# Loads, GLU tiles, sample states and chunks of a hybrid decoder step in another order, and expert rows in slots four apart

## The reference

```python
proj = xn @ w_in                               # z, xBC, dt, u
xbc, new_conv = _causal_conv(xbc, conv_prefix, conv_w, conv_b)
y, new_ssm = _ssd_chunked(xs, dt, -jnp.exp(a_log), bm, cm, d_ssd, ssm_h0, chunk)
y_ssd = _rmsnorm(y * jax.nn.silu(z), ssd_norm)
y_s5, new_re, new_im = _s5_group(u, ...)       # Re(C h) + D u, gelu, y * sigmoid(y @ w_glu), norm
x = x + jnp.concatenate([y_ssd, y_s5], axis=-1) @ w_out
x = x + _hier_moe(_rmsnorm(x, norm_ffn), ...)  # 4 groups x 8 experts, top 2 of one group
...
for e in range(MOE_EXPERTS):
    h = jax.nn.silu(t @ w_gate[e]) * (t @ w_up[e])
    out = out + gates[:, e:e + 1] * (h @ w_down[e])
```

## Time and profile before

| | us |
|---|---|
| median of 3 runs | 1102.85 |
| lowest, highest | 1101.57, 1104.02 |
| profiled execution | 1102.73 |
| its span | 1100.9 |
| TensorE busy | 992.9 (90%) |
| VectorE busy | 441.0 |
| ScalarE busy | 311.5 |
| GpSimd busy | 330.2 |
| waits of L650 for weights | 13.8 |
| L650, all wide tiles, busy | 273.1 |

### The profile page before, as it was taken

One profiled execution on the slowest core, in us unless ns is written; L12 is line 12 of the kernel. 1 busy time (PEld: TensorE's weight loads), 2 busy tenths in 40 slices (PEclk: granted clock), 3 DMA queues, 4 the chain that ended last, 5 costly groups with the idle time before them and its releaser, 6 DMA issues.

```text
span 1100.9 us, 16994 instructions
## 1 busy us (share of the span) xinstructions
PE 992.9 (90%) x6438; PEld 701.5 (64%) x6439; DVE 441.0 (40%) x674; ACT 311.5 (28%) x597; POOL 330.2 (30%) x534
## 2 busy tenths in 40 slices
PE   6999989999999999999999999999977778998881
PEld 5889768876876587999765555555544434554440
DVE  6999874353435699963151111111101011111103
ACT  3026222453202625322242222222212121221223
POOL 1000888888012994000012222222221111221210
PEclk9999999999979899999989999999989999999996
DMA  6684261110529643327299999999999999999954
GB/s 259 124 146 74 42 141 40 39 60 20 62 79 264 235 150 132 136 96 296 111 359 377 395 392 390 384 393 408 399 393 409 381 421 411 411 417 414 423 237 162
DMA packets 73564, 277.54 MB, mean 252 GB/s; under 512 B 36952, under 2 KB 38872, under 8 KB 56496
## 3 DMA queue, kind: packets, MB, share of 16 engines
q1 hardware_dynamic: 63020, 252.67, 62.6%
q0 software_dynamic: 8720, 19.86, 6.6%
q10 hardware_dynamic: 1780, 4.41, 1.1%
HBM read 260.17 MB, written 25.61 MB: 260 GB/s over the span
## 4 chain that ended last, share of the span: by engine, by line
PE 54%; DMA 22%; DVE 17%; SPq 3%; issue 2%; ACT 1%; POOLq 0%; ACTq 0%; POOL 0%; DVEq 0%
DMA sb_arena<-w_up 16%; PE ps L650 11%; PE ps L1015 8%; PE ps L1008 7%; PE ps L1029 7%; PE ps L912 7%; DVE sb_arena L1386 6%; DMA sb_arena<-w_gate 4%; SPq L407 2%; PE ps L982 2%; PE ps L769 2%; PE ps L795 1%; PE ps L820 1%; PE ps L738 1%; PE ps L816 1%
## 5 line engine op out<-in xcount | busy, mean ns | idle before, releaser
L650 PE MATMUL ps<-sb_arena 128*128 128x264 f32 (+1 forms) x1152 | 273.1, 398 | 14.7 <-DMA sb_arena<-wi 13.8
L650 PEld LDWEIGHTS ps<-sb_arena 128*128 128x128 f32 x1152 | 222.1, 194 | 65.9 <-DMA sb_arena<-wi 13.9
L1889 DVE TENSOR_TENSOR sb_s5b<-sb_s5b,ps 128x256 f32<-128x256 f32 x36 | 22.4, 623 | 414.4 <-PE ps L1015 414.4
L1015 PE MATMUL ps<-sb_arena 128*64 128x256 f32 x1152 | 134.5, 387 | 21.3 <-DMA sb_arena<-w_up 21.3
L1008 PE MATMUL ps<-sb_arena 128*64 128x256 f32 x1152 | 134.3, 387 | 19.1 <-DMA sb_arena<-w_gate 15.0
L1029 PE MATMUL ps<-sb_arena 128*64 128x512 f32 x576 | 131.5, 598 | 20.6 <-DVE sb_arena L1893 20.6
L1008 PEld LDWEIGHTS ps<-sb_arena 128*64 128x64 f32 x1152 | 84.3, 139 | 79.7 <-DMA sb_arena<-w_gate 24.4
L1015 PEld LDWEIGHTS ps<-sb_arena 128*64 128x64 f32 x1152 | 83.6, 139 | 68.3 <-DMA sb_arena<-w_up 27.4
L1359 ACT ACTIVATE sb_kxf<-ps,sb_gate_of 64x512 f32<-64x512 f32 x36 | 24.6, 682 | 304.9 <-PE ps L1029 304.9
L1029 PEld LDWEIGHTS ps<-sb_arena 128*64 128x64 f32 x576 | 39.0, 136 | 90.0 <-issue 61.0
L606 POOL COPY sb_idc<-sb_tok_of 64x1 int32 x36 | 6.4, 178 | 288.5 <-DMA sum_scr<-sb_kxf,sb_rwc 272.4
...
...
## 6 DMA issues: line engine op xcount, KB each, us to landing
...
sb_arena<-wi SPq DMA_DIRECT2D x28, 512.0 KB, 4.1
...
sb_arena<-wglu SPq DMA_DIRECT2D x8, 512.0 KB, 4.6
sb_arena<-ssm_in POOLq DMA_DIRECT2D x8, 512.0 KB, 15.3
o_ssm_s<-sb_arena POOLq DMA_DIRECT2D x8, 512.0 KB, 4.9
```

Source lines behind the costliest of these rows:

```text
L650: last = mm(ps[:, b0 + h, 0:t1 - t0], ring[w % 3][:, k, :], src[:, k, t0:t1], start=k == 0, stop=k == KD - 1)
L1015: last = mm(ps[64 * r:64 * r + 64, 1, 0:256], xt[:, k, :], Wu[s][:, k, 256 * r:256 * r + 256], start=k == 0, stop=k == KD - 1)
L1889: V.tensor_tensor(hh.rearrange("p (j c) -> p c j", j=2), sg.rearrange("p (c j) -> p c j", j=2), ps[:, 1, 0:256].rearrange("p (c j) -> p c ...
```

## The change

- The sync engine issues `ring_load(14)` after `toeplitz(0)` and 15 after `toeplitz(1)`; `y_load(0)` comes before `y_store(1)`.
- TensorE: `wide(25)` goes ahead of `state_outputs(0, 8)`, which now follows chunk 2's `ssd_y_off` and waits for `yo_ev` 4; `wide(27)` goes ahead of `ssd_c(3)`, `wide(28)` ahead of chunk 4, `wide(29)` ahead of `ssd_c(4)`. Tile 27 leaves bank 0 for the alternating pair.
- GpSimd loads samples 4 to 7 after the eighth round of state_outputs, bcf after the sixteenth, and samples 0 to 3 when all of `y_store(1)` has landed (`y5_st[1]`).
- VectorE: `off_diagonal` joins Yo and the decay of the carried state, ahead of the mask product (in chunk 4 ahead of the scaled inputs). The S5 additions 0 to 7 go into chunk 2 ahead of its y, 8 to 15 behind its states. Samples 0, 1, 2 are done in chunk 3 ahead of its y, 3, 4, 5 behind its states, 6 and 7 in chunk 4 ahead of its y. `project_out(3)` comes ahead of `root_inverse(1)`, `project_out(4)` between the two halves of `scale_s5`.
- ScalarE: the gelus come ahead of `b_tokens(4)` and `segment_exp(4)`, with a one-element Exp behind them, and read contiguous columns but write strided ones. The squares 4 to 7 move from tile 33 to 32.
- The slots: rank r = 16 e + w of a tile goes to slot 4 w + e.

```diff
         def wide_bank(w):
-            return 0 if 20 <= w < 28 else 2 * (w % 2)
+            return 0 if 20 <= w < 27 else 2 * (w % 2)
...
             toeplitz(0)
+            ring_load(14)
             toeplitz(1)
-            ring_load(14)
+            ring_load(15)
...
-            y_store(1)
             sp.wait_ge(y5_st[0], 16 * 9)
             y_load(0)
+            y_store(1)
             sp.wait_ge(y5_st[1], 16 * 9)
...
+            pl.wait_ge(y5_mm, 8)
+            for b in range(4, NS):
+                pl.dma_start(h0b[b], hin[b]).then_inc(h0s_ld[1], 16)
             pl.wait_ge(ea_out, 1)
             pl.wait_ge(y5_mm, 16)
...
-            for b in range(NS):
-                pl.dma_start(h0b[b], hin[b]).then_inc(h0s_ld[b // 4], 16)
+            pl.wait_ge(y5_st[1], 16 * 9)
+            for b in range(4):
+                pl.dma_start(h0b[b], hin[b]).then_inc(h0s_ld[0], 16)
...
             wide(24)
-            state_outputs(0, 8)
             ssd_a(2)
...
             wide(25)
+            pe.wait_ge(yo_ev, 4)
+            state_outputs(0, 8)
             ssd_c(2)
...
             wide(26)
+            pe.wait_ge(yo_ev, 6)
+            wide(27)
             ssd_c(3)
-            wide(27)
+            wide(28)
             ssd_a(4)
             ssd_b(4)
             ssd_y_off(4)
-            wide(28)
+            pe.wait_ge(yo_ev, 8)
+            wide(29)
             ssd_c(4)
-            for w in range(29, 36):
+            for w in range(30, 36):
...
+                if c == 2:
+                    s5_add(0)
+                for b in ((0, 1, 2) if c == 3 else (6, 7) if c == 4 else ()):
+                    sample_c(b)
                 dv.wait_ge(y_mm, c + 1)
...
+                if c == 2:
+                    s5_add(8)
                 if c == 3:
-                    sample_c(0)
-                    sample_c(1)
-            for b in range(4, NS):
-                sample_c(b)
+                    for b in range(3, 6):
+                        sample_c(b)
...
+            project_out(3)
             root_inverse(1)
             scale_s5(0)
+            project_out(4)
             scale_s5(1)
-            project_out(3)
-            project_out(4)
...
-            tt(oh_row, bc(flat(slf), 2, T), bc(io64, 1, 10), ALU.is_equal)
+            spread = lambda v: v.rearrange("p a (w e) -> p a w e", e=T // 16)
+            row_no = bc(io64.rearrange("p (e w) -> p w e", w=16), 1, 10)
+            rows_at = lambda: tt(spread(oh_row), spread(bc(flat(slf), 2, T)), row_no, ALU.is_equal)
+            rows_at()
```

More of the change, by code:

```diff
@@ L845, in _ @@
             wide(24)
-            state_outputs(0, 8)
             ssd_a(2)
-            pe.wait_ge(y5_ev, 8)
             ssd_b(2)
@@ L1206, in _ @@
             z_evac(20)
-            for c in range(5):
+            for c in range(4):
                 b_tokens(c)
@@ L1210, in _ @@
                     segment_exp(c)
-                if c < 4:
-                    decays(c + 1)
-                for w in ((21, 22), (23, 24), (25,), (26, 27), ())[c]:
+                decays(c + 1)
+                for w in ((21, 22), (23, 24), (25,), (26, 27))[c]:
                     z_evac(w)
@@ L1218, in _ @@
                     ac.wait_ge(yraw_ld[i // 4], 16)
-                act_(yg[:, i, 0:NP_].rearrange("p (m j) -> p m j", j=J),
-                     yraw[:, i, 0:NP_].rearrange("p (j m) -> p m j", j=J), ACT.Gelu_apprx_tanh)
+                act_(yg[:, i, 0:NP_].rearrange("p (m j) -> p j m", j=J),
+                     yraw[:, i, 0:NP_].rearrange("p (j m) -> p j m", j=J), ACT.Gelu_apprx_tanh)
                 act_(yg[:, i, NP_:N], yraw[:, i, NP_:N], ACT.Gelu_apprx_tanh).then_inc(gelu_done, 1)
+            link(act_(gate_of[:, 0:1], ones[:, 0:1], ACT.Exp))
+            b_tokens(4)
+            segment_exp(4)
             for i in range(2):
@@ L1623, in _, with s5_add, off_diagonal @@
             Ug = U[:, 0:G5 * UC].rearrange("p (g c) -> p g c", g=G5)
+            def s5_add(first):
+                for rd in range(first, first + 8):
+                    dv.wait_ge(y5_mm, rd + 1)
+                    o = Ug[:, 4 * rd:4 * rd + 4, 0:YC]
+                    V.tensor_tensor(o, o, ps[:, 2 + rd % 2, 0:4 * WIN].rearrange("p (q c) -> p q c", q=4)[:, :, 0:YC],
+                                    ALU.add).then_inc(y5_ev, 1)
+            def off_diagonal(c, n):
+                for g in range(2):
+                    dv.wait_ge(yo_mm, 2 * c - 1 + g)
+                    V.tensor_tensor(Yo[0:n, 8 * g:8 * g + 8, :],
+                                    ps[0:n, 2 + g, :].rearrange("p (h d) -> p h d", d=HD),
+                                    bc(dE[0:n, c, 0, 8 * g:8 * g + 8], 2, HD), ALU.mult).then_inc(yo_ev, 1)
+                for g in range(2):
+                    hs = Hs[:, 8 * g:8 * g + 8, :]
+                    tt(hs, hs, bc(dE[:, c, 1, 8 * g:8 * g + 8], 2, HD), ALU.mult)
             for c in range(5):
```

28 lines of the change are left out of this document (8 added, 20 removed).

## The result

The changed kernel took 1106.74 us (median of 10 runs, 1104.28 to 1111.38) against 1102.41 of the kernel before (10 runs, 1099.32 to 1104.02): a ratio of 1.0054, 95% interval 1.0041 to 1.0067, so **0.54% slower**, some 6 us by the ratio and 4.3 by the medians. The two differ because six runs of the changed kernel lie at 1104 to 1107 and four at 1111. The profiled execution took 1106.85 with a span of 1105.0, 4.1 longer than that of before.

What follows compares the result with a forecast made beforehand. TensorE was taken to bound the front (150 to 480 us), the expert weight stream 780 to 1052. From 1102.73 us, the front's -3.7 and the slots' +4.1 gave 1103.1, range 1092 to 1110.

Steps and rivals of the forecast that it cites:

- The gap at tile 15: Wide tiles 15 and 16: the 5.14 us weight wait and 2.67 of half clock go, TensorE 7.8 us earlier.
- Chunks 2 and 3: Up to ssd_c(3): a 1.3 us wait for the S5 additions and 6.0 of half clock go; end at 341.0.
- The GLU's first tile: Tile w28 waits for gelus behind y_store(1) and y_load(1): +2.8 us (0 to +6).
- Chunk 4 behind the samples: ssd_a(4) waits on VectorE, where samples 0 to 2 precede chunk 3's y evacuation: +7.6 us (0 to +12).
- the rival called slower: Sample states 0 to 3 land after 350, idling TensorE at ssd_a(4): about 1111 us, or 1107; chance 0.15.
- Tile 29: w29 waits for chunk 4's Yo, which stands behind samples 3 to 5 on VectorE: +4.9 us (2 to 6).
- The clock: TensorE's clock halves after the new gaps of 2.8, 7.6 and 4.9: three losses of 2.9, +8.8 us (2.7 to 13).
- The end of the front: VectorE's y_lo ready at about 426, so its 2.07 us wait goes; first projection block at 434.9 instead of 434.37.
- -1.7 and -2.5: Output projection: 1.7 us of half clock at the first block goes, and TensorE's 2.49 wait at project_out(3).
- Front in all: First block +0.5, then -1.7 and -2.5 behind it: -3.7 us (-9 to +6).
- The slots: Expert gathers and scatters: two neighbouring slots to an engine, fullest engine 109 rows instead of 99: +4.1 us.
- The rival of four slots to an engine: Four neighbouring slots share a DMA engine, so new slots level the rows: 1080 to 1093, 1087 us; chance 0.08.

Runs made afterwards that it cites:

- d4: The changed kernel with ring_load(14) and (15) back where they had been, 15 behind all Toeplitz transfers: 1115.3 us, ratio 1.0119 to the kernel before.
- b3: The kernel before with only project_out(3) and (4) moved as in the change: 1099.53 us, ratio 0.9973.
- a1: The kernel before with the new slots alone: 1105.15 us, ratio 1.0039.
- a3: The changed kernel with the old slots (rank r to slot r): 1102.69 us, ratio 1.0015 to the kernel before.
- c0: The changed kernel with samples 0 to 3 in chunk 4 behind its mask product, 4 to 7 behind its states: 1106.6 us, ratio 1.0045 to the kernel before.
- d2: The changed kernel, samples 0-3 loaded without waiting for y_store(1), slots 32h+2w+e, samples 0-3 behind chunk 4's mask product, 4-7 behind its states: 1104.93 us, ratio 1.0031.

## Why the prediction was right, and where it was not

The forecast was 1103.1 with a range of 1092 to 1110, that is +0.4 on the kernel before; 1106.74 lies in the range. Its likeliest class (faster than 1100.6, 0.42) did not come; what came, slower than 1105, had been given 0.30, and no change 0.28. That the front's sum came so near is partly luck: VectorE's chain, put at 426, was ready only at 434.66, which happens to be where TensorE was forecast to arrive (434.9). By its own steps:

- **The gap at tile 15**: 7.8 expected, the two tiles end 8.7 earlier, of which 0.9 was there before them. d4 gives the step 7 to 8.6 us of the whole. (The Toeplitz transfers are 32 in the timelines, eight to a call, and not the 64 of the description; the prediction's sixteen and eight fit that.)
- **Chunks 2 and 3**: ssd_c(3) was to end at 341.0 and ended at 340.3; no wait, no half clock.
- **The GLU's first tile**: +2.8 expected, 0 came. y_store(1) landed at 335.1, as worked out (335), but y_load(1) took 5.1 us and not 11, and the gelus were done at 344.4.
- **Chunk 4 behind the samples**: this is the term that was mis-sized, +7.6 expected, 15.66 measured. 2.8 of it is the wait at tile 28 that did not come, and 0.7 that TensorE was there earlier. 4.5 is the landing of samples 0 to 3: 347.5 expected (345 to 351), 351.95 measured. The estimate counted 3 MB, the samples and y_load(1), but not the two GLU tiles and w_out; from 334 to 352 us the engines moved 5.37 MB. That these loads are the cause is the likeliest reading, and no run moves them away. Late samples were the mechanism of the rival called slower, whose point of decision (350) was passed. (The parts of the sum, 347.5, 7.4, 2.2 and 1.4, give 358.5 and not 358.9.)
- **Tile 29**: +4.9 expected, 3.24.
- **The clock**: 8.8 was expected for three gaps, and the lengths give about 8.5, an estimate from rows such as 9.18 for 7.39 at tile 29. But it is not three gaps: the first did not come, and about 3.4 of it is the fall at 388, behind ssd_c(4) and no wait. The prediction had taken off this very loss (5.1, at 373.5 to 383.7) as one that goes; it moved with ssd_c(4).
- **The end of the front**: VectorE's y_lo was to be ready at 426 and was ready at 434.66. First block: 434.9 expected, 437.30. **-1.7 and -2.5** behind it: -3.8 in the trace (from +2.9 to -0.9), and b3 has the second alone, as 2.3 in its trace and 3.0 in its time. Front in all: -3.7 expected, -0.9 measured.
- **The slots**: +4.1 expected, +5.3 in the trace, 4.3 in a1, about 4 between a3 and the changed kernel, and 4.9 by the means of the table. The mapping read from seven rows was right, and the two other maps were told apart as said. The upper end, the count of rows times the price of a row (5.8), was nearer than the lower end (2), a third of it. The rival of four slots to an engine had been priced at 6.3 to 18.6 us faster; by its own rule the fullest engine would go from 140 rows to 86, which is 31 at the same price.

What the sum did not have at all: the first block could hardly start before 435 whatever TensorE waited for. In the changed kernel y_lo is ready at 434.66, so of all the waits of TensorE no more than about 2.5 us reach the block, and in c0, where they are gone (and sample 0 stands 5 us later), it starts at 435.82. From sample 0 on VectorE has next to no idle time, and GpSimd's 75 us stand beside it and stretch it. The prediction counted VectorE's chain as ready at 426 with two samples instead of six left, and took GpSimd for no part of it; c0 and d2 show that it ends with GpSimd's. The gain of 7.8 and of 7.3 more in chunks 2 and 3 went there: TensorE came to the sixteenth round 14 us earlier, and the loads behind y_store(1) gave back all of it.
